# Hybrid decoder layer: the input projection's job pairs as seven block products, with DeltaNet's steps on a grid of their own

## What is computed

```python
proj = xn @ w_in                       # (1024, 1024) @ (1024, 6408)
aq, ak, av, dqkv, dbeta, da, dz, gate_a, gate_b = split(proj)
# A: 3 groups of 4 heads of width 64, (window, dilation) = (128,1), (512,4), (2048,16);
#    softmax attention over t, t-d, ..; groups weighted by their softmax denominators
# B: short causal conv + silu on dqkv, q/k normalised, chunked delta rule:
#    v_new = u_i - w_i @ state;  o_i = qd_i @ state + qk_i @ v_new
#    state = state * gl_i + kd_i.T @ v_new
y = sigmoid(gate_a) * (o_a @ w_pa) + sigmoid(gate_b) * (o_b @ w_pb)
h = x + y @ w_o
out = rms_norm(h + conv_glu_ffn(rms_norm(h)))
```

## Time and profile before

| | |
|---|---|
| median of 3 runs | 1611.21 us (1611.08 to 1611.26) |
| span of the profiled execution | 1610.9 us |
| PE busy | 1583.4 us, 98%, 7913 instructions |
| DVE / ACT / POOL busy | 885.1 / 580.8 / 641.8 us |
| chain that ended last | PE 92%, DVE 5%, DMA 2% |
| stages, roughly | head to 45 us, projection to 803 to 805, merge and output projection to 965, FFN to the end |

### The profile page before, as it was taken

One profiled execution on the slowest core, in us unless ns is written; L12 is line 12 of the kernel. 1 busy time (PEld: TensorE's weight loads), 2 busy tenths in 40 slices (PEclk: granted clock), 3 DMA queues, 4 the chain that ended last, 5 costly groups with the idle time before them and its releaser, 6 DMA issues.

```text
span 1610.9 us, 20471 instructions
## 1 busy us (share of the span) xinstructions
PE 1583.4 (98%) x7913; PEld 1321.1 (82%) x7913; DVE 885.1 (55%) x1326; ACT 580.8 (36%) x857; POOL 641.8 (40%) x471
## 2 busy tenths in 40 slices
PE   6999999999999999999999999999999999999998
PEld 4888888888888888888788887888888888878886
DVE  5232321454535353566554148756666566788886
ACT  4422222132322254333222134444444444444445
POOL 3333422312121223224324347987778888100111
PEclk9999999999999999999999999999999999999999
DMA  5222352221313142445457031432233432697685
GB/s 173 66 79 84 100 159 65 54 70 52 79 42 88 34 138 45 133 128 152 137 205 261 14 114 33 135 92 92 92 98 113 123 118 84 232 314 234 199 263 183
DMA packets 206444, 196.47 MB, mean 122 GB/s; under 512 B 23524, under 2 KB 157196, under 8 KB 206348
## 3 DMA queue, kind: packets, MB, share of 16 engines
q1 hardware_dynamic: 206128, 195.08, 39.2%
q10 hardware_dynamic: 220, 0.09, 0.0%
HBM read 146.76 MB, written 48.37 MB: 121 GB/s over the span
## 4 chain that ended last, share of the span: by engine, by line
PE 92%; DVE 5%; DMA 2%; issue 1%; ACT 1%; SPq 0%; POOL 0%; DVEq 0%; ACTq 0%
PE acc L566 37%; PE acc L2507 12%; PE bank_ab L1442 7%; PE bank_ab L2507 7%; PE acc L2517 6%; PE att_ps L2507 5%; PE bank_ab L2517 3%; PE acc L1877 3%; PE att_ps L2517 3%; PE att_ps L1523 2%; PE bank_ab L1877 1%; PE att_ps L1877 1%; PE att_ps L1505 1%; DMA f_raw<-in_w_down_dram 1%; DVE u_t_full L1833 1%; PE att_ps L1516 1%
## 5 line engine op out<-in xcount | busy, mean ns | idle before, releaser
L566 PE MATMUL acc<-xh,w_high 128*128 128x512 f32 x832 | 274.0, 406 | 0.6 <-POOL xl L1766 0.6
L566 PE MATMUL acc<-xl,w_high 128*128 128x512 f32 x832 | 262.3, 392 | 0.0
L1007 POOL TENSOR_TENSOR w_low<-w_raw,w_high 128x1024 fp32r<-128x1024 f32 x49 | 117.4, 2395 | 363.1 <-ACT w_high L1085 363.1
L566 PE MATMUL acc<-xh,w_low 128*128 128x512 f32 x832 | 261.3, 390 | 0.0
L566 PEld LDWEIGHTS acc<-xh,w_low 128*128 128x128 f32 x832 | 156.6, 188 | 34.3
L566 PEld LDWEIGHTS acc<-xl,w_high 128*128 128x128 f32 x832 | 156.5, 188 | 33.8
L566 PEld LDWEIGHTS acc<-xh,w_high 128*128 128x128 f32 x832 | 146.9, 189 | 23.9 <-POOL xl L1766 1.0
L1179 ACT ACTIVATE sc<-sc,mx 128x128 f32<-128x128 f32 (+1 forms) x96 | 35.5, 441 | 172.3 <-DVE mx L1386 172.3
L1279 DVE SCALAR_TENSOR_TENSOR cs<-acc,prm,cs 128x1023 f32<-128x1023 f32 (+2 forms) x36 | 46.1, 1282 | 79.5 <-ACT cs L1103 78.6
L2283 POOL TENSOR_TENSOR f_h<-f_h,f_fw 128x512 f32<-128x512 f32 x8 | 11.0, 1369 | 170.5 <-ACT f_junk L2206 170.5
L2517 PE MATMUL acc<-f_w_high,f_gh 128*128 128x512 f32 x176 | 68.8, 391 | 0.0
(11 more groups left out here) (391 smaller groups left out, 3807.8 us busy)
## 6 DMA issues: line engine op xcount, KB each, us to landing
w_raw<-in_w_in_dram SPq DMA_DIRECT2D x51, 512.0 KB, 4.6
f_raw<-glu_d SPq DMA_DIRECT2D x66, 256.0 KB, 3.1
f_raw<-in_w_down_dram SPq DMA_DIRECT2D x55, 256.0 KB, 4.2
w_raw<-in_w_up_dram SPq DMA_DIRECT2D x24, 512.0 KB, 5.1
glu_d<-u_free_high SPq DMA_DIRECT2D x22, 512.0 KB, 4.6
u_raw_even<-in_w_up_dram SPq DMA_DIRECT2D x20, 512.0 KB, 4.7
f_raw<-gsum_d SPq DMA_DIRECT2D x33, 256.0 KB, 3.6
conv_d<-so SPq DMA_DIRECT2D x16, 512.0 KB, 3.0
```

What stands on the lines that cost most here:

```text
L566: mm = nc.tensor.matmul(out[:, lo:hi], w, xx[:, lo:hi], start=first and j == 0, stop=last and j == 2)
L1007: g.tensor_tensor(wl[:, n % 2], raw[:, n % 2], wh[:, n % 2].bitcast(F32), ALU.subtract).then_inc(s_wlo, 1)
```

## The change

48 of the 51 jobs are taken in 24 pairs. A pair's weights are a 2 x 2 arrangement of blocks (two jobs, two halves of K), and so are the columns of x (two halves of K, two halves of columns). Seven products of 4 K tiles by 512 columns by three matmuls replace eight such: 84 matmuls for 96. Three jobs stay plain (`PLAIN`).

- The differences of blocks of x (`t_full`, `t_high`, `t_low`) are formed once, in the head and the first jobs. For them `norm_head` keeps the second half of x unsplit (`second`).
- Per pair POOL forms four sums of weight blocks (`add_up`), ACT and POOL split seven blocks into high and low (`split`), in a ring of three (`RING`), and DVE and ACT mix the products (`one`, `two`, `three`, `four`).
- Weights are loaded in four blocks a pair. q, k, v and gates go through one staging tile to DRAM (`att_d`, `gate_d`); attention units load their own q, k and v again (`aload`), and V is transposed per unit (`a_v` and behind `a_pv`).
- A slot is now three matmuls. `ATT_GAP` = 6, 4, 2 slots. DeltaNet's steps stand every `DN_GAP` = 3 slots from pair 5 on, whatever attention does. The groups of attention are taken from dilation 16 to dilation 1, and combining runs beside the last group's units.
- The squares of the norms move from POOL to ACT; the masks move from the head to pairs 0 to 4; o goes to DRAM and is loaded and split in the last two pairs; two pairs of gates stay in SBUF; the first branch weights have a place of their own.
- Memory places are fixed numbers. In the merge and the FFN only places and semaphores change.

```diff
+GROUP_ORDER = (2, 1, 0)
+DIRECT_GATES = 2
+PLAIN = 3
+NP = 7
+HK = KT // 2
+RING = 3
+TURN = NP * HK
...
+    for p in range(pairs):
+        first, second = pair_jobs(p)
+        for i in range(NP):
+            for k in range(HK):
+                slot = p * TURN + i * HK + k
+                items.append(("mp", p, i, k))
...
+                if key == (4, 1):
+                    items += [("split", p, 6), ("raw", p + 1, 1)]
+                    if p + 1 < pairs:
+                        items += [("sum", p + 1, 1), ("sum", p + 1, 2)]
+                if key == (5, 0):
+                    items.append(("evac", first))
+                if key == (5, 1) and p + 1 < pairs:
+                    items += [("split", p + 1, 0), ("sum", p + 1, 3)]
+                if key == (6, 1) and p + 1 < pairs:
+                    items += [("split", p + 1, 1), ("sum", p + 1, 4)]
+                if p < 5 and key == (2, 2):
+                    items.append(("masks", p))
+                if kind == "conv" and t == 2 * NH:
+                    items += {(5, 2): [("rnorm",)]}.get(key, [])
...
+                if dn and slot >= DN_FROM and slot >= dn_slot + DN_GAP:
+                    dn_slot = slot
...
+ATT_GAP = {"a_v": 3, "a_qk": 6, "a_pT": 4, "a_pv": 2}
+DN_GAP = 3
+DN_FROM = 5 * TURN + 2 * HK
+TAIL_AT = (4, 0)
...
+                if kind == "two":
+                    dve.wait_ge(s_prod, NP * p + 2)
+                    dve.wait_ge(s_one, 2 * p + 1)
+                    g.tensor_tensor(two, one, x[:, rest_cols], ALU.add).then_inc(s_mix, 1)
...
+                if kind == "split":
+                    n = NP * it[1] + it[2]
+                    pool.wait_ge(s_vhi, n + 1)
+                    g.tensor_tensor(vl[n % RING], source[it[2]], vh[n % RING].bitcast(F32),
+                                    ALU.subtract).then_inc(s_vlo, 1)
```

1000 lines of the change are left out of this document (635 added, 365 removed).

## The result

The changed kernel takes 1673.95 us (median of 4 runs, 1671.07 to 1678.70) where the kernel before, run beside it, takes 1611.14: a ratio of 1.0394, 95% interval 1.0375 to 1.0413. It is slower by 63 us; the forecast was 30 us faster. Its profiled execution spans 1677.0 us (it is the slowest of the four), that of before 1610.9.

What follows compares the result with a forecast made beforehand. TensorE was taken to bound the projection stretch. 288 fewer matmuls save 65.3 us, 35.7 comes back, and the remaining 29.6 off 1611.2 gives 1581.6 us, with an 8-in-10 range of 1560 to 1604.

Steps and rivals of the forecast that it cites:

- DeltaNet's hand-walk: DeltaNet steps in the projection: following DVE's queue, TensorE waits 1.3 us a chunk, 10 us for eight chunks.
- the reckoning of the combining by DVE's load: Combining beside the last eight attention units: DVE 90% loaded, costing 4 us, bounds 0 to 12.
- low clock: After the pause at POOL's power, TensorE's clock is low for a while, costing 1.4 us.
- the untouched FFN: FFN after the projection: untouched by the change and as long as before, with no cost in the sum.
- power: Pair 4: POOL's 10.57 us power of the inverse norms delays a low part, so TensorE stands 10.3 us.
- head: Start of the kernel: extra copies by ACT and differences of blocks on POOL and DVE cost 1 us, 0 to 5.
- convolution pairs: Five convolution pairs: emptying an accumulator takes 5.3 us of the 5.44 allowed, costing 1 us, 0 to 5.
- attention: 24 attention units: the path from scores to probabilities mostly fits, costing 0.25 us a unit, 6 us.
- tail: Pair 22: loading six tiles and the branch weights delays a block its last sum wants, costing 2 us, 0 to 6.
- (b): Rival: POOL becomes a second bound in the projection, low parts blocked for 19 us more, 1601 us; chance 0.20.
- (a): Rival: the other engines hide nearly all but the power, 53 us saved, 1558, taken as 1560 us; chance 0.15.
- (c): Rival: ACT is held at each attention unit for the whole 7.2 us before the exponentials, 1697 us; chance 0.05.

Runs made afterwards that it cites:

- combine_sums_only: The changed kernel without the weights of the combining, DVE doing only the two sums of the three outputs (attention output not the reference's): 1645.44 us.
- combine_later: The changed kernel with each unit's combining three slots later, behind the next unit's scores, and its transposes five slots later: 1674.67 us.
- combine_next_slot: The changed kernel with each unit's combining one slot later, behind the output's copy, its load three slots and its transposes one slot later: 1668.10 us.
- no_long_vector_block: The changed kernel with power in four, inverse later, tiles at old offsets plus 512 bytes, without combining weights or inverse arithmetic, head sums behind DVE's scalings: 1590.12 us.

## Why the prediction was wrong

The saving was right, and so nearly is the pace of 2.72 us for 12 matmuls: where nothing waits and nothing stands between, a product takes 2.72 to 2.79 us. What failed is the list of what comes back: 35.7 us in the sum, 131.4 measured (78.2 + 46.2 + 7.0). Within it the steps that failed are DeltaNet's hand-walk (10 us; 18.4 by the place of one block), the reckoning of the combining by DVE's load (4 us; 28.5 by leaving it out), the low clock charged once (1.4 us; up to 32.6) and the untouched FFN (nothing; 10.6). Point by point:

| term | in the sum | measured |
|---|---|---|
| power | 10.3 + 1.4 | 10.0, and 1.9 of slow matmuls behind it |
| head | 1 | 8, if the first pair was due at 65 us: it starts at 73.1 (65.7 to 73.5 over the runs) |
| convolution pairs | 1 | none: pairs 1 to 3 take 22.9 and 23.0 us with no wait of over 0.35 us |
| DeltaNet | 10 | 18.4 by the inverse's place alone |
| attention | 6 | about 11 of waits for the copy in combine_sums_only, 560 to 830 us |
| combining | 4 (0 to 12) | 28.5 by leaving its weights out |
| tail | 2 | 2.5 in two waits for low parts |
| place in memory | not there | 10.6 |
| low clock behind waits | 1.4, once | at most 32.6 (15 stretches) |

The measured column doesn't add up to 131.4: what a run gives back holds the low clock behind its waits too, so the rows overlap.

**Power, convolution pairs, tail.** Right, the power to 0.3 us and by the walk through POOL's queue that the prediction gives. It is the one place where the queue was followed instruction by instruction with what stands ahead of each.

**DeltaNet's grid.** "1.3 us a chunk" is the term that was mis-sized. The hand-walk has the two large products of the inverse (1.46 and 1.14 us) and no term for its first part, the 13 small steps ahead of the emptying of P6: 3.05 us in the kernel before, 3.0 to 7.9 here. And it started the inverse when its turn came, without the wait for a DMA at its head, for which DVE stood 11.7 us in the first chunk (9.85 us of TensorE) and 3.4 in the second; in the trace of before DVE stood 12.3 us there in the first chunk (to 231.1 us), and TensorE had no wait of over 0.3 us near it. A wait in an in-order queue holds what stands behind it like an instruction; I counted only instructions.

**Durations beside POOL.** The terms for DVE are means from a trace in which POOL was busy 215 of 757.5 us. In the changed kernel it is 434.7 of 816.6. Comparing each DVE instruction of the projection with the shortest of its kind, 68 are longer by over 0.1 us, 57 us in all, against 29 and 40 us before; line 1716 above took 1.07 us for 12 columns where it takes 0.17 undisturbed. As a load that is little, 17 us in 816.6, and the large instructions were hardly dearer than the prediction has them (combining's products 0.63 us in the mean for its 0.73, the inverse's 1.22 and 1.18 for 1.46 and 1.14). What it missed is where the extra lies: in the many small steps of the inverse and the combining, each of which can wait out one of POOL's instructions, so that a block of 3 us takes 4 to 8. What that costs the kernel no run prices. The prediction gave this rule as a load on POOL, in rival (b), but not on DVE, where it bit: POOL's own low parts stayed at 1.32 us in the mean.

**Combining.** The step that failed is the reckoning by load: "90%" of DVE's time, and so 4 us. DVE was at 63%. Nor was the amount of work under-estimated: the prediction has 15.4 us of DVE a unit, and 99.66 us for eight are 12.5 (72% even of the 17.2 us that it gives a unit). What counts is how soon the thing behind the block is wanted. TensorE wants the copy of a unit's output two slots of three matmuls after the values, 1.4 us and the steps there, and a product sum must be emptied within two products, 5.44 us by the prediction's own convolution term; a combining is one block of 3.0 to 6.9 us. At neither of the two other places that were tried, combine_later and combine_next_slot, did it fit as a whole.

**Low clock.** The prediction charged it once, behind the power, 1.4 us. It was granted at half in 15 stretches of the projection, each at a wait of over 2.3 us, 88.7 us long with TensorE busy for 65.3 of them: at most 32.6 us of the 46.2 by which TensorE's busy time is above the sum's.

**FFN and merging.** "FFN is untouched" is true of its code and false of its time, since the change moved its tiles.

**The rivals.** (a), all hidden, no. (b), POOL as second bound, no: apart from the power TensorE waits some 5 us for low parts. (c) named ACT behind the softmax and 1697 us; the time is near, the mechanism is another. ACT's wait for DVE's maximum even fell, from 172.3 us to 108.0. So (c)'s time is luck; what it had right is an in-order queue that holds what TensorE wants, but on the wrong engine.

What stays open: in no_long_vector_block there are still 32.7 us of waits and 16.5 us of busy time above the sum's (704.6 less 688.1; at most 7 of it low clock) in the projection. The largest single ones are 7.0 us for the gates in the head, which is this run's own, and 11.3 us in eight waits for low parts. The rest are many of under 3 us, which no run took apart.

## What to carry to other kernels

Before taking work off the bounding engine, list for each in-order queue the longest stretch, waits for DMAs included, that stands ahead of something the bounding engine wants, and compare it with how long that engine's prepared work lasts; the mean load says little (63% here, and 28 us lost). Count a chain of small DVE instructions with both inputs in SBUF at what it can take beside a busy POOL, not at its undisturbed time (here up to 7.9 us for 3.05). Work that was harmless as one block may need cutting when the pace quickens, and longer waits are paid again as slow matmuls (here at most 32.6 us on top of 82.3 of waits). And a change that moves tiles is a change of every stage that reads them: compare the pace of untouched stages first.
